# Router logits from the raw x, and the second half of the tokens selected inside the first expert pass

## The reference, cut to what matters

```python
xp = layer_norm(ALPHA * xp + mp[2] * m_p, ln1_g[l], ln1_b[l])
hp = modulate(xp, mp[3], mp[4])              # x * (1 + scale) + shift
...
def moe_swiglu(h, router, wg, wu, wd):
    probs = jax.nn.softmax((h @ router).astype(jnp.float32), axis=-1)
    top_v, top_i = lax.top_k(probs, TOP_K)   # 2 of 8
    top_v = top_v / jnp.sum(top_v, axis=-1, keepdims=True)
    gates = ...
    for e in range(N_EXPERTS):
        out = out + gates[..., e:e + 1] * swiglu(h, wg[e], wu[e], wd[e])
```

## Time and profile before

| | |
|---|---|
| median of 3 runs | 1141.8 us (1141.01 to 1142.6) |
| the profiled execution | 1143.45 us |
| its span | 1141.7 us |
| TensorE's mean granted clock | 0.995 |
| DMA | 335.77 MB, mean 294 GB/s |

### The profile page before, as it was taken

The page is one execution under the profiler, slowest core; times in us unless marked ns, Lnnn a source line. Parts: engine busy times, 40 slices in busy tenths (PEclk is TensorE's granted clock), DMA queues, the critical chain, the costliest instruction groups (busy, mean ns, idle before and its releaser), DMA issues.

```text
span 1141.7 us, 15874 instructions
## 1 busy us (share of the span) xinstructions
PE 1121.8 (98%) x5614; PEld 896.6 (79%) x5614; DVE 865.5 (76%) x1271; ACT 695.2 (61%) x1020; POOL 89.9 (8%) x125
## 2 busy tenths in 40 slices
PE   6999999999999999999999999999999999999998
PEld 4666767777689889777777888788888888888885
DVE  5668667756775455677867766789999999999997
ACT  4544446533744444465555644578887888878884
POOL 4100100000070000000000002011011010000010
PEclk9999999999999999999999999899999999999999
DMA  9998883699759947496664557499999999999991
GB/s 335 334 352 305 329 322 135 221 322 342 249 169 415 328 151 239 156 360 222 209 197 148 191 191 266 163 350 386 395 385 400 374 406 400 389 403 376 386 399 63
DMA packets 142731, 335.77 MB, mean 294 GB/s; under 512 B 6856, under 2 KB 35752, under 8 KB 142672
## 3 DMA queue, kind: packets, MB, share of 16 engines
q1 hardware_dynamic: 133152, 304.11, 73.2%
q0 software_dynamic: 9344, 30.82, 7.8%
q10 hardware_dynamic: 176, 0.07, 0.0%
HBM read 317.63 MB, written 17.33 MB: 293 GB/s over the span
## 4 chain that ended last, share of the span: by engine, by line
PE 90%; DVE 5%; ACT 2%; DMA 1%; issue 1%; POOL 0%; ACTq 0%; DVEq 0%
PE bank L1679 26%; PE bank L1681 26%; PE bank L1680 26%; PE bank L1918 2%; PE bank L2020 1%; DVE w_lo L1067 1%; PE bank L2038 1%; PE bank L1848 1%; PE bank L2028 1%; DMA lamv<-in_lam_k 1%; PE bank L1952 1%; PE bank L1837 1%; DMA work<-in_ln_in_b 1%; ACT w_hi L709 0%; PE bank L1797 0%
## 5 line engine op out<-in xcount | busy, mean ns | idle before, releaser
L1067 DVE TENSOR_TENSOR w_lo<-raw,w_hi 128x1024 fp32r<-128x1024 f32 (+1 forms) x492 | 567.0, 1179 | 176.5 <-ACT w_hi L709 171.7
L709 ACT ACTIVATE w_hi<-raw 128x1024 fp32r<-128x1024 f32 (+1 forms) x492 | 490.5, 1008 | 298.9 <-PE bank L1681 281.5
L1679 PE MATMUL bank<-w_hi,xT_hi 128*128 128x512 f32 (+1 forms) x1056 | 412.7, 391 | 3.2 <-DVE w_lo L1067 1.5
L1681 PE MATMUL bank<-w_lo,xT_hi 128*128 128x512 f32 (+1 forms) x1056 | 402.7, 381 | 0.0
L1680 PE MATMUL bank<-w_hi,xT_lo 128*128 128x512 f32 (+1 forms) x1056 | 401.6, 380 | 0.0
L1679 PEld LDWEIGHTS bank<-w_hi,xT_hi 128*128 128x128 f32 x1056 | 199.7, 189 | 46.3 <-DVE w_lo L1067 6.3
L1681 PEld LDWEIGHTS bank<-w_lo,xT_hi 128*128 128x128 f32 x1056 | 198.6, 188 | 35.6
L1680 PEld LDWEIGHTS bank<-w_hi,xT_lo 128*128 128x128 f32 x1056 | 199.0, 188 | 31.1
L1679 PE MATMUL bank<-w_hi,hT_hi 128*128 128x512 f32 x360 | 142.9, 397 | 0.1
L1681 PE MATMUL bank<-w_lo,hT_hi 128*128 128x512 f32 x360 | 140.4, 390 | 0.0
L1680 PE MATMUL bank<-w_hi,hT_lo 128*128 128x512 f32 x360 | 140.4, 390 | 0.0
(11 more groups left out here) (290 smaller groups left out, 864.3 us busy)
## 6 DMA issues: line engine op xcount, KB each, us to landing
raw<-in_w_in SPq DMA_DIRECT2D x46, 1024.0 KB, 7.5
raw<-in_ada_w SPq DMA_DIRECT2D x41, 1024.0 KB, 8.2
raw<-in_moe_w_down SPq DMA_DIRECT2D x40, 1024.0 KB, 9.1
raw<-in_moe_w_gate SPq DMA_DIRECT2D x32, 1024.0 KB, 8.4
raw<-in_moe_w_up SPq DMA_DIRECT2D x32, 1024.0 KB, 7.8
raw<-in_moe_w_gate SPq DMA_DIRECT2D x16, 768.0 KB
raw<-in_moe_w_up SPq DMA_DIRECT2D x16, 768.0 KB, 9.3
raw<-in_w_attn_out SPq DMA_DIRECT2D x8, 1024.0 KB, 5.0
```

Of the source, the lines that this page charges most:

```text
L709: nc.scalar.activation(w_hi[:, unit, 0:n], raw[:, r, at:at + n], ACT.Copy).then_inc(hi_done, 1)
L1067: V.tensor_tensor(w_lo[:, unit, 0:n], raw[:, r, at:at + n], w_hi[:, unit, 0:n].bitcast(F32), ALU.subtract).then_inc(lo_done, 1)
L1679: pe.matmul(o, hi, wh, start=start, stop=False)
L1681: return pe.matmul(o, hi, wl, start=False, stop=stop)
```

## The change

Router columns are scaled in advance: VectorE multiplies `r_raw` by `modA` and `modB` (`r_coef`), and TensorE sums both over the channels with `all_ones` ahead of the slot products. The router's products take x as it is after the residual, turned (`raw_turned`, copied by `raw_turned_kept` into the place of `tokens`); `route` applies rstd and nmr. ScalarE gets a list of its own, `to_experts`, in place of `to_next` for this norm. The tokens go by halves of the channels: the first half of both groups is turned, copied and selected ahead of the first pass; the second half inside its first slot, by `second_half`, which `row_units` calls behind each unit. The late half-blocks are spread (one, two, and one inside the slot) and use bank 7; idle products are 2, 5 and 3 instead of 3. GpSimd's scatter waits for all four copies of tokens.

The diff, without semaphore names and lines that only follow (`LATE_BANK`, the loops of `modulate` and `transpose_xhat`, which take a half or a range, and a copy moved from `places` to `first_tokens`):

```diff
+        r_coef = sb("r_coef", [P, KD, 2, G, NE])
+        r_sums = sb("r_sums", [P, 2, G, NE])
...
+        raw_xT = tokens.rearrange("p g (k t) -> p g k t", t=T)
...
+        TOKEN_BANKS = ((6, 4), (4, 5))
+        LATE_BANK = 7
...
+            def raw_turned_kept(i):
+                act.wait_ge(raw_t, i + 1)
+                nc.scalar.activation(raw_xT[:, i // 2, i % 2 * 4:i % 2 * 4 + 4, :], four(bank[4 + i]), ACT.Copy).then_inc(raw_kept, 1)
+
+            def token_half(g, half):
+                order = 2 * half + g
+                act.wait_ge(xt_t, order + 1)
+                nc.scalar.activation(tokens[:, g, half * COL:(half + 1) * COL], bank[TOKEN_BANKS[half][g]][:, :], ACT.Copy).then_inc(xt_ok, 1)
+
+            def first_gathered(half):
+                act.wait_ge((sel_half, gx_t)[half], 1)
+                nc.scalar.activation(xT_hi[:, 4 * half:4 * half + 4, 0, :], four(bank[half]), ACT.Copy).then_inc(gx_hi, 1)
+
+            def to_experts(n, q):
+
+                nc.scalar.activation(sd[:, G:G + 1], eps_c[:, 0:1], ACT.Sqrt)
+                hi(q, 0, (0,))
+                ln_std(n, 0)
+                ln_scale(n, 0)
+                hi(q, 0, (1,))
+                for i in range(2 * G):
+                    raw_turned_kept(i)
+                ln_std(n, 1)
+                act.wait_ge(coef_ok, n)
+                modulate(n, 0)
+                ln_scale(n, 1)
+                modulate(n, 1)
+                token_half(0, 0)
+                token_half(1, 0)
+                modulate(n, 0, 1)
+                first_gathered(0)
+                hi(q, 0, (2, 3))
+                token_half(0, 1)
+                ada_copy(len(GROUPS) - 1)
+                token_half(1, 1)
+                first_gathered(1)
+                act.wait_ge(r_max, 1)
+                nc.scalar.activation(rs[:, 2, :], rs[:, 2, :], ACT.Exp).then_inc(r_exp, 1)
+                act.sem_inc(y_sent, 16)
...
-                    nc.scalar.activation(slot_no, bank[2][:, P:2 * P], ACT.Copy).then_inc(slot_ok, 1)
+                    nc.scalar.activation(slot_no, bank[2][:, P:2 * P], ACT.Copy)
+                    nc.scalar.activation(r_sums[:, :, :, :].rearrange("p w g e -> p (w g e)"), bank[2][:, 0:2 * G * NE], ACT.Copy)\
+                        .then_inc(slot_ok, 1)
...
+                    to_experts(3, q0)
...
+                    if n == 2 * DEPTH - 2:
+                        dve.sem_inc(x_half, 1)
...
-                    modulate(n + 1, 0)
-                    lo(q + 1, 0, (0,))
-                    modulate(n + 1, 1)
-                    lo(q + 1, 0, (1,))
...
+                dve.wait_ge(slot_ok, 1)
+                dve.wait_ge(nmr_ok, G * 2 * DEPTH)
+                for g in range(G):
+                    ins = V.scalar_tensor_tensor(out=rt[:, 3, g, :], in0=r_sums[:, 0, g, :], scalar=nmr[:, g:g + 1],
+                                                 in1=r_sums[:, 1, g, :], op0=ALU.mult, op1=ALU.add)
+                then(ins)
...
-                then(V.tensor_copy(E(0), bank[2][:, 0:G * NE].rearrange("p (g e) -> p g e", g=G)))
+                for g in range(G):
+                    ins = V.scalar_tensor_tensor(out=rt[:, 0, g, :], in0=bank[2][:, g * NE:(g + 1) * NE], scalar=rstd[:, g:g + 1],
+                                                 in1=rt[:, 3, g, :], op0=ALU.mult, op1=ALU.add)
+                then(ins)
...
+                if l:
+                    dve.wait_ge(ld_small, 32)
+                    for w, mod in enumerate((modA, modB)):
+                        for g in range(G):
+                            ins = V.tensor_tensor(r_coef[:, :, w, g, :], r_raw[:, :, :],
+                                                  mod[:, 3, :, g].unsqueeze(2).to_broadcast([P, KD, NE]), ALU.mult)
+                    ins.then_inc(r_coef_ok, 1)
...
                     first_tokens()
+                    lo(q0, 0, (0, 1))
+                    gathered(0, (0,))
+                    modulate(3, 1)
+                    lo(q0, 0, (2, 3))
                     places()
-                    gathered(0, (0,))
-                    lo(q0, 0, (2,))
                     gathered(0, (1,))
-                    lo(q0, 0, (3,))
                     one_pass(q0, 0, False, {1: late_kept, 2: passes, 4: gates})
                     last_pass = dve.value_load(plan[0:1, 0:1], min_val=NE - 1, max_val=PASSES - 1)
                     with dve.Fori(1, last_pass) as p:
...
+                    if after:
+                        after(unit)
...
+                    pe.wait_ge(r_coef_ok, 1)
+                    for k in range(KD):
+                        pe.matmul(bank[2][:, 0:2 * G * NE], all_ones[:, :], r_coef[:, k, :, :, :].rearrange("p w g e -> p (w g e)"),
+                                  start=k == 0, stop=k == KD - 1)
                     pe.matmul(bank[2][:, P:2 * P], all_ones[:, :], before[:, :], start=True, stop=False)
                     pe.matmul(bank[2][:, P:2 * P], all_ones[:, :], ident[:, :], start=False, stop=True).then_inc(slot_mm, 1)
                 pe.wait_ge(m_ok, 4 * l + 4)
...
                     ada_turn(group_of(OUT_QUAD), bank[2][:, :])
                 rows_by_group(q0 + 1, 2, xT_hi, xT_lo, 4, 8)
                 q0 += 2
-                transpose_xhat(2 * l + 1, 0)
-                if l:
-                    for n_half in late_halves[0:2]:
-                        ada_half(n_half)
-                    pe.wait_ge(slot_ok, 1)
                 if l == 0:
+                    transpose_xhat(1, 0)
                     for e in range(DENSE_PARTS):
                         expert(q0 + e * Q_EXPERT, e, e == 0, e == DENSE_PARTS - 1, None if e else 1)
                 else:
+                    def raw_turned(g, half):
+                        pe.wait_ge(x_half, 2 * g + half + 1)
+                        for k in range(4):
+                            ins = pe.transpose(bank[4 + 2 * g + half][:, k * T:(k + 1) * T],
+                                               x[:, g, (4 * half + k) * P:(4 * half + k + 1) * P], ident[:, :])
+                        ins.then_inc(raw_t, 1)
+
                     def routed(g, half):
-                        pe.wait_ge((mod_act, mod_dve)[half], G * 2 + g + 1)
+                        pe.wait_ge(raw_kept, 2 * g + half + 1)
                         for k in range(4 * half, 4 * half + 4):
-                            ins = pe.matmul(bank[2][:, g * NE:(g + 1) * NE], modulated[:, g, k, :], r_raw[:, k, :],
+                            ins = pe.matmul(bank[2][:, g * NE:(g + 1) * NE], raw_xT[:, g, k, :], r_coef[:, k, 0, g, :],
                                             start=k == 0, stop=k == KD - 1)
                         return ins
 
                     def tokens_turned(g, half):
                         for k in range(4):
-                            ins = pe.transpose(bank[(6, 4)[g] + half][:, k * T:(k + 1) * T], modulated[:, g, 4 * half + k, :], ident[:, :])
+                            ins = pe.transpose(bank[TOKEN_BANKS[half][g]][:, k * T:(k + 1) * T], modulated[:, g, 4 * half + k, :], ident[:, :])
                         ins.then_inc(xt_t, 1)
 
-                    pe.wait_ge(ld_small, 32)
+                    def selected(half):
+                        for k in range(4 * half, 4 * half + 4):
+                            for g in range(G):
+                                ins = pe.matmul(bank[half][:, (k % 4) * T:(k % 4 + 1) * T], tokens[:, g, k * P:(k + 1) * P],
+                                                first_sel[:, g, :], start=g == 0, stop=g == G - 1)
+                        return ins
+
+                    def second_half(unit):
+                        if unit == 0:
+                            ada_half(late_halves[3])
+                            pe.wait_ge(mod_act, G * 2 + 3)
+                            tokens_turned(0, 1)
+                        if unit == 1:
+                            pe.wait_ge(mod_dve, G * 2 + 1)
+                            tokens_turned(1, 1)
+                        if unit == 2:
+                            pe.wait_ge(xt_ok, 2 * G)
+                            selected(1).then_inc(gx_t, 1)
+
+                    raw_turned(0, 0)
+                    raw_turned(0, 1)
+                    raw_turned(1, 0)
+                    transpose_xhat(3, 0, range(0, 4))
+                    idle_products(2, 2)
+                    raw_turned(1, 1)
                     routed(0, 0)
-                    transpose_xhat(3, 1)
                     routed(0, 1)
-                    tokens_turned(0, 0)
                     routed(1, 0)
                     routed(1, 1).then_inc(r_col, 1)
-                    tokens_turned(0, 1)
-                    tokens_turned(1, 0)
-                    tokens_turned(1, 1)
-                    for n_half in late_halves[2:4]:
-                        ada_half(n_half)
+                    transpose_xhat(3, 0, range(4, 8))
+                    idle_products(5, 3)
+                    transpose_xhat(3, 1)
```

(42 more changed lines are left out.)

46 lines of the change are left out of this document (15 added, 31 removed).

## The result

The changed kernel takes 1150.41 us (median of 5, 1149.32 to 1151.99), against 1141.8 before (1141.01 to 1144.9): ratio 1.0074, interval 1.0056 to 1.0091. The forecast was 1147.5, slower with a chance of 0.86. The direction is right; the median is 2.9 above the forecast and lies on the upper end of the range, 1150.4. The profiled execution took 1149.32 (span 1147.5, mean clock 0.998). It is the fastest of the five: the others took 1150.30 to 1151.99, at clocks of 0.995 to 0.997.

A forecast was written before the change was run, and what follows sets the result against it. TensorE was taken as the bound, its 20.35 us stretch ahead of the experts partly at half clock. 1.8 + 0.25 + 0.85 + 3.05 - 0.25 = +5.7 us on the median 1141.8 gave 1147.5, range 1143.6 to 1150.4.

The forecast's parts named there:

- Sums: Ahead of the slot products: eight products with all_ones, 16 loads, all on TensorE's path, +1.8 us (bounds 1.4 to 3.5).
- The copy of `r_sums`: On ScalarE ahead of the split of the last output slot's unit 2: +0.25 us (0.2 to 0.4).
- Logits: Router on raw x: VectorE takes logits at 727.55 instead of 731.65, mask ready 3.9 us earlier; old time, 2.05 added later.
- TensorE's list up to the second slot, without the wait: TensorE's work from 720.87: 26.8 us plus one 0.5 wait, ending at 748.2 against 747.35, +0.85.
- The wait: Ahead of the second slot, TensorE stands 3.05 us for ScalarE's copy, table load, Exp and split, then VectorE's rest.
- The profiled execution: Counterpart of the profiled execution before, which took 1143.45 us: forecast 1149.15.
- What later waits take up: Waits of 0.74 at 758.85 and 0.43 at 765.27 were to give back 0.25 us (0 to 1.2).
- From one execution to the median: Whole kernel: the +5.7 us counted on one profiled execution was added to the median 1141.8, giving 1147.5.
- The first rival: Clock falls again behind the router pairs, some 15 pairs at 0.22 instead of 0.115: +1.6, 1149.1; chance 0.25.
- No stall: Rival: stall ahead of the second slot absent or absorbed by an earlier wait or later ones: 1144.7; chance 0.12.
- cheap pairs: Rival: small pairs among 512-column products hide their loads: 1144.0 at 0.09 us a pair, 1139.7 at 0.06; chance 0.14 with other gains.
- The rule on transposes: Around the router pairs: if transposes don't count as TensorE activity, the clock's fall would be nearly certain.

The follow-up runs named there:

- the filled wait: Changed kernel with twelve idle products behind the turn, in TensorE's wait ahead of the second slot: median 1151.27 us, ratio 1.0086.
- the packed one: Changed kernel with second-slot units split early, sums reduced on VectorE, no idle products, two late half-blocks behind the router pairs: median 1144.39 us, ratio 1.0027.
- early split: Changed kernel with ScalarE splitting units 0 to 2 of the second slot before the second selection's copy and Exp: median 1149.2 us, ratio 1.0063.

## Why the prediction was right in direction and short in size

- **Sums:** +1.8 forecast, 16 loads in 1.99 and 1.8 of delay measured, and 1.56 given back by the reduction to two pairs. Right. The copy of `r_sums` was put at 0.25; TensorE's wait for unit 2 grew from 0.25 to 0.35, and the table of the two profiles has +0.1.
- **Logits:** at VectorE 729.6 forecast, 729.07 measured. Right.
- **TensorE's list up to the second slot, without the wait:** 748.2 plus 2.05, so 750.25, forecast; 748.85 measured (turn at 748.28 and its 0.57). The first product, forecast at 740.3, came at 739.05. Of the 1.4, the start was 0.3 early and the copy 0.15 cheaper; the ten idle products took 1.93 instead of 2.3, the first slot and its turn 5.6 instead of 5.9, the router pairs 3.49 instead of 3.68, and the wait was 0.42 instead of 0.5. The half-blocks took 4.38 from the end of the load before each, where 4.43 was counted. The transposes took 0.1 more, and the rest ran as counted.
- **The wait:** 3.05 forecast, 2.89 measured, with the chain as described (copy 0.60, table 1.28, Exp 0.20, split). Right, and shown by the two kernels that shorten it to 1.39 and to nothing.
- **Clock in the wait:** the step left it out. "TensorE stands 3.05 us" was priced as time alone; the clock fell behind it, +1.4. Shown by the filled wait.
- **The profiled execution:** 1149.15 was forecast and 1149.32 came, but that is partly luck: 1.4 counted too much for the start, the copy and the list stood against the 1.4 of the clock, which nobody had priced.
- **What later waits take up:** 0.25 was given back; the waits of 0.74 and 0.43 stand unchanged after, so 0.
- **From one execution to the median:** this is the step that failed. "its counterpart would be 1149.15" came out at 1149.32. But "the median 1141.8 + 5.7" did not hold. The difference was made against an execution whose stretch ran partly at the half clock, and for a changed order without that fall. Yet the kernel before has that fall in only part of its executions: the slices from 726 to 736 lose 3.4 us of full clock, 0.003 of the mean, and 25 of 69 ran at a clock of 1.000. "That is the gain, 3.9 us, and the half-clock stretch is behind most of it" took for the change's own what before has by itself whenever the clock stays up. From the old order at full clock (24.22 with four idle products more; these take 0.7 in their rows, and 1.2 by the executions at a clock of 1.000, so 23.0 to 23.5 without) the stretch of the change, without its wait, is 2.9 to 3.4 longer. So where before keeps the full clock, the new order costs 1.9 (sums and copy) + 3.2 + 2.9 + 1.4 = 9.4. At like mean clocks both sides have lost as much to falls, so the 1.4 drops out, which leaves 8.0: the table has 7.8 to 8.4. For the medians, an estimate: 9.4, plus 1.6 for a fall behind the router pairs, less the 2.5 that 1141.8 lies above the 1139.3 of a full clock, makes 8.5, and 8.6 was measured. No execution of the kernel before at the full clock has a trace, and of the change's five only the profiled one has, so the distribution of clocks carries this part.
- **The first rival** (the clock falls again behind the router pairs; 1149.1) was given 0.25. Of the seven profiles with 32 pairs in one piece ahead of idle products or transposes besides the change's own, six show it (all but the packed one), at a cost of 1.6 or 3.2 in the stretch. The change's own other four executions have lower clocks than the profiled one, which fits; they have no trace, and a fall near 65 or at the end would do the same. It should have been the likelier case. With the clock behind the wait it is 1149.1 + 1.4 = 1150.5, which is the median; but this stands on the same step from one execution to the median, and so meets it partly by luck.
- **No stall, cheap pairs:** both out. The pairs took 0.11 to 0.12 each, among 512-column products too (16 in 1.98 at 745.11). A reserve of up to 1.2 in the later waits wasn't there.
- **The rule on transposes** (the Trainium skill, "TensorE: Matmul & The Clock Gate", Part 4: they don't count as TensorE activity in the same way) made the fall nearly certain. It didn't happen in the change's profile nor in the packed one's, and did in six others with nearly the same order: a statement of likelihood fits these traces, certainty doesn't.

What the 3.2 is made of can be counted from rows. There are 16 more transposes (1.9), and seven more idle products, which the change itself put in (1.35: ten in 1.93, where before has three in 0.58). The lines of before and after:

```profile
737.19 0.54 PEld L1691 LDWEIGHTS bank<-idle 128*128 128x128 f32 x3
```

```profile
729.19 1.00 PEld L1740 LDWEIGHTS bank<-idle 128*128 128x128 f32 x5
```

The kernel without idle products bears this out: less 1.7 for its fall, its stretch is 25.0 where the early split has 26.4, though its wait for ScalarE's copies is 0.92 and no longer 0.42. Smaller terms of both signs are left.

What stays open: why the same program keeps the clock in one execution and loses it in the next; why five executions of the early split took 2 to 5 us more than its profiled one; and whether idle products raise the share of executions that keep the clock.

## What to carry to other kernels

Before a change is priced against one profiled execution, look whether that execution ran at a granted clock below its siblings', and where: a stretch at the half clock is no gain to be had in the executions that don't have it. A wait on TensorE ahead of a dense stream costs its own length and the slower products behind it; 2.9 us of standing cost 4.3 here. And splitting work into halves to start the dense stream earlier helps only if the in-order engine that feeds the next slot isn't left with the second half, a table load and the split in a row.

## What was not expected of the hardware

- The clock falls by execution, not by program: the kernel before spread over 1138.6 to 1146.0 in 69 executions, at mean clocks of 1.000 to 0.994, a quarter and more of them (25) at 1.000. The traces show half-clock stretches in four places: near 65 (before, and one other of thirteen traces), behind the router products near 728, behind the wait ahead of the second slot, and 6 to 11 us ahead of the end (five traces).
- Twelve idle products in 2.60 us kept the clock (one trace) through a wait in which standing still lost it (two traces); a wait of 1.39 us didn't lose it (one trace). With idle products among thin pairs the clock was full in three profiles of four, but the executions at 1.000 were no more frequent for it, other than in the packed order (two of eight, against none of twelve).
- Behind products of 32 columns (the late half-blocks) the next full load stands 0.84 us each time: at 732.86, 739.05 and 741.63 in the change, as at 723.92 and 736.08 before. Each place where a half-block is put costs this once: from the end of the load before it, a single one took 1.16 and 1.35, a pair 1.87 (2.03 before). So scattering them costs more than doing them together.
